# One block for output projection and feed-forward, with the superblocks' ends in another order, in a decoder layer on one Trainium2 core

## What is computed

```python
mixed = jnp.concatenate([y_rwkv, y_pool], axis=-1).astype(x.dtype) @ w_out[layer]
x = x + rms_norm(mixed, post_mix_norm[layer])
h = rms_norm(x, pre_ffn_norm[layer])
f = conv_ffn(h, w_up[layer], conv_w[layer], conv_b[layer], w_down[layer])
x = x + rms_norm(f, post_ffn_norm[layer])
```

## Time and profile before

| | us |
|---|---|
| median of 3 runs | 2393.16 |
| lowest, highest | 2385.60, 2395.46 |
| the profiled execution, its own time | 2396.97 |
| its span, from first to last instruction | 2395.2 |
| TensorE busy in it | 2245.9 (94%) |
| VectorE, ScalarE, GpSimd busy | 1764.1, 1144.1, 1017.4 |
| granted TensorE clock, mean | 0.975 |

### The profile page before, as it was taken

One profiled execution on the slowest core, in us unless ns is written; L12 is line 12 of the kernel. 1 busy time (PEld: TensorE's weight loads), 2 busy tenths in 40 slices (PEclk: granted clock), 3 DMA queues, 4 the chain that ended last, 5 costly groups with the idle time before them and its releaser, 6 DMA issues.

```text
span 2395.2 us, 43619 instructions
## 1 busy us (share of the span) xinstructions
PE 2245.9 (94%) x16652; PEld 1825.7 (76%) x16652; DVE 1764.1 (74%) x1905; ACT 1144.1 (48%) x1794; POOL 1017.4 (42%) x726
## 2 busy tenths in 40 slices
PE   6999999996999989987999999999899999999997
PEld 5777777775878767776888888788678888887885
DVE  2656797984785466767999998656689899976457
ACT  4646565542445444444444444454444444444434
POOL 3646465571333245434677776200136555541000
PEclk9999999997999889998999999999999999999999
DMA  6364555456567357884334344678633233326666
GB/s 186 100 222 131 196 153 184 132 166 164 159 173 195 109 153 237 256 266 145 127 110 144 122 145 136 215 243 257 221 111 114 95 116 100 102 93 206 193 220 211
DMA packets 435787, 395.61 MB, mean 165 GB/s; under 512 B 59516, under 2 KB 352044, under 8 KB 432300
## 3 DMA queue, kind: packets, MB, share of 16 engines
q1 hardware_dynamic: 407772, 343.06, 46.5%
q10 hardware_dynamic: 27856, 50.34, 6.0%
HBM read 266.97 MB, written 126.35 MB: 164 GB/s over the span
## 4 chain that ended last, share of the span: by engine, by line
PE 46%; DVE 3%; DMA 2%; issue 1%; ACT 1%; POOL 1%; SPq 0%; ACTq 0%; DVEq 0%; POOLq 0%
PE late_bank L135 16%; PE late_bank L137 15%; PE late_bank L136 15%; DVE wt_lo L2773 1%; DMA raw<-scratch_td 1%; DVE p_ub L2801 0%; DMA p_keep<-in_w_down 0%; DMA scratch_td<-p_keep 0%; DVE wt_lo L2729 0%; DMA raw<-in_w_down 0%; ACT wt_hi L2613 0%; ACT late_bank L2630 0%; DVE p_ub L2738 0%; DVE p_ub L2804 0%; DVE p_keep L2801 0%
## 5 line engine op out<-in xcount | busy, mean ns | idle before, releaser
L135 PE MATMUL late_bank<-o_hi,wt_hi 128*128 128x512 f32 x1232 | 482.8, 392 | 13.5 <-DVE p_ub L2738 6.1
L136 PE MATMUL late_bank<-o_lo,wt_hi 128*128 128x512 f32 x1232 | 482.1, 391 | 0.0
L137 PE MATMUL late_bank<-o_hi,wt_lo 128*128 128x512 f32 x1232 | 482.0, 391 | 0.0
L428 POOL TENSOR_TENSOR p_w_lo<-p_w_raw,p_w_hi 128x1024 fp32r<-128x1024 f32 x72 | 189.9, 2638 | 223.9 <-ACT p_w_hi L496 223.9
L135 PEld LDWEIGHTS late_bank<-o_hi,wt_hi 128*128 128x128 f32 x1232 | 233.1, 189 | 63.6 <-issue 8.6
L136 PEld LDWEIGHTS late_bank<-o_lo,wt_hi 128*128 128x128 f32 x1232 | 233.0, 189 | 48.7
L137 PEld LDWEIGHTS late_bank<-o_hi,wt_lo 128*128 128x128 f32 x1232 | 232.9, 189 | 48.6
L135 PE MATMUL late_bank<-wt_hi 128*128 128x512 f32 x616 | 242.3, 393 | 16.2 <-DVE wt_lo L2773 15.2
L2493 POOL TENSOR_TENSOR tsum<-raw 128x512 f32<-128x512 f32 x43 | 102.9, 2394 | 363.5 <-DMA out<-tsum 195.0
L136 PE MATMUL late_bank<-wt_lo,wt_hi 128*128 128x512 f32 x616 | 240.8, 391 | 0.0
L137 PE MATMUL late_bank<-wt_hi,wt_lo 128*128 128x512 f32 x616 | 240.7, 391 | 0.0
(11 more groups left out here) (314 smaller groups left out, 4613.1 us busy)
## 6 DMA issues: line engine op xcount, KB each, us to landing
raw<-in_w_up SPq DMA_DIRECT2D x88, 512.0 KB, 5.1
p_w_raw<-in_w_in SPq DMA_DIRECT2D x72, 512.0 KB, 3.9
scratch_a<-p_keep SPq DMA_DIRECT2D x22, 1280.0 KB, 4.6
raw<-scratch_a SPq DMA_DIRECT2D x104, 256.0 KB, 2.9
raw<-scratch_td SPq DMA_DIRECT2D x60, 256.0 KB, 3.6
p_keep<-scratch_a SPq DMA_DIRECT2D x50, 256.0 KB, 2.9
scratch_a<-p_keep SPq DMA_DIRECT2D x44, 256.0 KB, 2.0
raw<-in_w_down SPq DMA_DIRECT2D x44, 256.0 KB, 3.9
```

What stands on the lines that cost most here:

```text
L135: nc.tensor.matmul(out, lhs_hi, rhs_hi, start=start, stop=False, skip_group_check=again)
L136: nc.tensor.matmul(out, lhs_hi, rhs_lo, start=False, stop=False, skip_group_check=again)
L137: return nc.tensor.matmul(out, lhs_lo, rhs_hi, start=False, stop=stop, skip_group_check=again)
L428: nc.gpsimd.tensor_tensor(w_lo[i][:, :, :], w_raw[i][:, :, :], w_hi[i][:, :, :].bitcast(F32), ALU.subtract).then_inc(s_wl, 1)
```

## The change

Both phases become one block (`phase_out_and_ffn`): `mix_out_programs` returns the five programs, which run ahead of the feed-forward's own on each engine, with no barrier or credit block between; the feed-forward's semaphores are credited by SP behind the second tile.

```diff
+            body(0, 0)
+            body(1, 1)
+            for s in credited:
+                sp.sem_inc(s, ONE)
+            for t in range(2, N):
+                body(t, t % 2)
             begin_next()
```

```diff
-                    sp.wait_ge(s_op, ONE + N)
+                sp.wait_ge(s_wl, ONE + 1)
                 for ph in range(EARLY_OPERANDS, OPERANDS):
+                    if ph == 5:
+                        store_quarters(sp, N // 2 - 2)
+                        sp.wait_ge(s_op, ONE + N)
...
+                if t == N - 1:
+                    for k in range(KT):
+                        for n in range(HALF):
+                            last = nc.tensor.matmul(bank[:, 2 * p + n, :], m_hi[p][:, k, :], w_lo[:, k, n * TB:(n + 1) * TB],
+                                                    start=k == 0, stop=False)
+                    last.then_inc(s_wl, 1)
...
+                if t == N - 1:
+                    for ph in (3, 4):
+                        unit_high(ph)
+                        operand_high(ph)
+                    first_copy()
                 act.wait_ge(s_x2, ONE + t + 1)
...
+                if t == N - 1:
+                    unit_high(5)
+                    operand_high(5)
                 act.wait_ge(s_rc, ONE + t * 2 + 2)
```

```diff
+                if p and t < N - 1:
+                    second_root(t, p)
                 if 2 < t <= N // 2 + 1 and p:
                     first_low((t - 3) // 2)
...
                         else:
                             load_step(sup, 0)
                             load_step(sup, 1)
+                        if sup == 0 and u == 0:
+                            mix.store_quarters(sp, N_TILES // 2 - 1)
+                            for p in range(2):
+                                sp.wait_ge(mix.x_stored[p], ONE + N_TILES * 8)
+                                sp.wait_ge(mix.pieces_stored[p], ONE + PIECES * 8)
+                        if sup == 0 and u == 1:
+                            sp.wait_ge(s_qst, ONE + QUARTERS)
+                            load_piece(0)
...
-                        if begins(n) and ph == 0:
+                        if begins(n) and ph == 4:
+                            mix.transposes(pe, N_TILES - 1, 1)
+                        if begins(n) and ph == 5:
+                            pe.wait_ge(mix.turned, ONE + N_TILES)
```

```diff
+        ORDER = (2, 3, 0, 1)
...
-                            piece_sums(h - 2)
+                            piece_sums(h - 1)
...
-                    if ph == PH - 1 and f % 2 and f < 2 * TT:
-                        norm(sup, 0, f // 2)
+                    if ending(sup) and e == RUN:
+                        for t in range(TT):
+                            norm(sup, 0, t)
+                    elif not ending(sup) and ph == PH - 1 and 0 < f <= 2 * TT:
+                        if f % 2:
+                            scaled(sup, 0, f // 2)
+                        else:
+                            added(sup, 0, f // 2 - 1)
...
                 for t in range(TT):
                     last_combine(SUPERS - 1, t)
-                for t in range(TT):
                     norm(SUPERS - 1, 1, t)
```

```diff
+        LAST_PARTS = {14 + 4 * f: f for f in range(FP)}
+        RUN = STEPS - FP
...
+                def last_product(sup):
+                    ph = PH - 1
+                    for t in range(TT):
+                        pe.wait_ge(s_es, ONE + sup * 5 * TT + 2 * TT + t + 1)
+                        for f in range(FP):
+                            if t == 0:
+                                pe.wait_ge(s_ol, ONE + PH - EARLY_OPERANDS + KQ * PH + f + 1)
+                            hi, lo = whole(f, o_hi), whole(f, o_lo)
+                            end = split_matmul(nc, bank[:, BASE[ph] + t, :], hi[:, t * P:(t + 1) * P], lo[:, t * P:(t + 1) * P],
+                                               hi[:, TB:2 * TB], lo[:, TB:2 * TB], False, f == FP - 1, True)
+                        end.then_inc(s_db if t < TT - 1 else s_dp, 1)
```

686 lines of the change are left out of this document (380 added, 306 removed).

## The result

The changed kernel takes **2360.2 us** (median of 4 runs, 2355.37 to 2364.81), the kernel before beside it 2393.26 (4 runs, 2385.6 to 2395.46): ratio 0.986, 95% interval 0.9839 to 0.9881. The forecast was 2346.0 in 2336 to 2359. The sign is right; the size falls short by 14.2 us, and the range misses by 1.2.

What follows compares the result with a forecast made beforehand. TensorE, busy 2245.9 of 2395.2 us, was taken as the bound, so only its waits, low clock and the tail could be won. Six terms sum to 47.2 us, giving 2346.0 against the median 2393.16, range 2336 to 2359.

Steps and rivals of the forecast that it cites:

- Part 1: Output projection, odd tiles: an earlier second reciprocal on VectorE removes four TensorE waits for the scaled tile, -5.8 us.
- Part 2: Projection's end and first unit: the stop between phases goes, 44.5 us becomes 29.5, -15 (bounds -23.7 and -10).
- the second unit near 1091: End of the walk past the projection: the second unit begins near 1091 us instead of 1106.
- queue rival: The full DMA queue, not the block, sets the projection's boundary: -10 there, 2351 us in all; chance 0.17.
- Part 3: First superblock's 77 steps: earlier pieces and a norm cut in two, 223.2 to 215.9 us, -7.3 (-5 to -8.5).
- the first term: First superblock's steps: last piece's store no longer precedes the third step load; its 4.6 us wait goes, 3.8 expected.
- Part 4: Between the superblocks: tiles 2 and 3 first, addition ahead of the norm, -10.5 us (bounds -5.6 and -13).
- backlog rival: VectorE's packed units move the start waits by a unit, 5 and 2 us back, 2353 us; chance 0.13.
- Part 5: Second superblock's last product: step operands loaded and split earlier, four waits at the end go, -2.3 us.
- the ring was not choked: Slower rival, second superblock's steps: early last parts hold back step loads, +63 us, 2409; chance 0.02.
- Part 6: Tail behind the last matmul: norms tile by tile cut 14.5 us to 8.2, -6.3 (-5 to -7).

Runs made afterwards that it cites:

- u1: Changed kernel with VectorE's second reciprocal of odd tiles back behind the copies and the turn; 2365.58 us, ratio 0.9885.
- q1: Changed kernel with the second unit's raw weights loaded ahead of operand 6 instead of behind it; 2347.58 us, ratio 0.9798.
- e1: Changed kernel with the last pair's sums on VectorE moved behind the first addition of the second unit; 2354.57 us, ratio 0.9835.
- n1: Changed kernel with the last tile pair's sums on VectorE cut to one column, giving a wrong result; 2356.61 us, ratio 0.9852.
- gn: g1 with the last tile pair's sums on VectorE also cut to one column, giving a wrong result; 2349.75 us, ratio 0.982.
- h1: g1 with the load queue reordered: second unit's raw weights, sums' store, operands 5 and 6, then small parameters; 2349.58 us, ratio 0.9817.
- o1: Changed kernel with the tiles of the steps in the old order 0, 1, 2, 3; 2359.33 us, ratio 0.9858.
- p1: Changed kernel with the pieces of the down projection's weight sums one pair of units later again; 2356.35 us, ratio 0.9839.
- e2: Changed kernel with ScalarE's store of the first superblock's fourth tile behind the copies of the next unit's first weights; 2354.10 us, ratio 0.9817.
- u2: Changed kernel with the second superblock's last product back in eleven ring steps, norm halves between, no early parts; 2367.99 us, ratio 0.9886.
- g1: q1 with the 512 KB load of the last norm's gain also moved later, into the second unit; 2351.09 us, ratio 0.9819.

## Why the prediction was wrong in size

The miss of 14.2 us (2346.0 to 2360.2) has three parts: 5.5 from the parts of the sum (47.2 forecast, 41.7 in stretches A to F), 3.1 from ahead of stretch A, and 5.6 from where the profiled executions lie among the others: I set the sum against an execution 3.8 us above its median, and the one after stands 1.8 below its own. The last two are scatter, and the forecast had no term for it; without them its sum would have missed by 5.5 us and its range would have held.

*Part 1: right.* -7.1 for -5.8; u1 brings back four waits. The rest is TensorE's own busy time in A, 168.6 us before and 167.4 after, for which the sum had no term.

*Part 2: the step that failed, -15 forecast, -10.5 measured.* Its first half went better than my walk. Counted from the projection's end, operand 5 was copied after 13.7 us (I had 14.5), product 6 began after 24.3 (26.5), and the second unit after 27.0 (29.5). But I let the walk end there. The mis-sized term is "the second unit near 1091", after which I counted no loss: the next unit's raw weights stood last on the crowded queue, the sums I had moved in stood ahead of the additions, and the second unit lost 6.9 us (33.9 of B's 434.1 lie ahead of the 400.2 for 21 units, and 33.9 - 27.0 = 6.9; 5.46 of it waited, the rest at the lower clock). q1 shows the queue's part, 3.6 of them. e1, n1 and gn show the sums' part to be under 1 us, by place or by amount. The other 3.3 us I can't assign: with the weights first (q1) operand 6 is late, in h1's order GpSimd's sums run beside VectorE's low halves, and every such version keeps B at 429.5 to 431.6. So the **queue rival** came nearest: it gave -10 and named "the first unit's raw weights among them"; it was the second unit's. That its figure fits within 0.5 us is partly luck, since it is the sum of a first unit that came 2.5 us sooner than I had it and a second that lost 6.9. Its reason, volume, is only half shown: order gained 3.6 us, and taking out 512 KB that stood behind the late operand gained nothing more. The Trainium skill (Trainium Kernel Development and Optimization, "Key Constraints") says that all queues run on one set of engines, and this trace's DMA share of 1.00 to 1.09 between 1065 and 1080 agrees. What I drew from it, that loads set sooner gain nothing, doesn't fit: operands 3 and 4 were copied 1.0 and 3.4 us behind the projection's end, 11.9 and 15.9 before.

*Part 3: -5.6 for -7.3.* The start waits are 3.8 us, as forecast. The end waits are 2.3 us where I left 0.3: a norm in two halves fits the ring, but GpSimd's sums, moved beside them by part 4, make VectorE's 1.2 us instructions 2.3 (o1, without them, has C at 214.6). By waits and clock, C's 5.6 us are 1.9 of start waits (5.7 to 3.8), 1.1 of end waits (3.4 to 2.3) and 2.4 of clock: 0.83 in 1506.1 to 1520 before, behind the one long wait, 1.00 after. My reason for the first term is too simple: p1 puts the piece's store back ahead of the load, which brings 1.0 us of start waits (4.8 us) and 0.6 us of C, within the noise. The kernel before had the same store and 5.7 us of waits because there it came later still. Both kernels issue the load 3 us behind the store; but GpSimd's four piece sums, which the store waits for, took 5.7 us before (1501.56 to 1507.26) and 4.9 in p1 (1484.62 to 1489.54), and began 4.5 us ahead of the first step instead of 5.4. These two make up the 1.6 us between the two loads; why the sums began and ran later, no run shows.

*Part 4: -8.6 for -10.5.* The chain was as read, and by o1's trace the order is worth more than I gave it. The terms for what is left were both wrong, and it is luck that they nearly cancel: I put 0.4 us ahead of the first product, where there are 2.77, with the clock at 0.78 in 1709 to 1715 on top, and 2.6 us for a wait further on, where there is none. The sum also forgot its own 0.4: 13.1 - 0.4 - 2.6 is 10.1. e2 shows the backlog rival in small: with ScalarE out of the way, VectorE's combine is late by 1.63.

*Part 5: -3.6 for -2.3*, the ring was not choked: no wait at the eleven new parts. The four waits went, but not for the reason given, that no norm stands between low halves: u2, with the norm's halves between them, has none of the four either, and its E is 0.4 us longer. The term was right and its reason was not; the cut in two is the likely one, which no run undoes alone. *Part 6: -6.4 for -6.3.*

The range took one rival at a time, on top of a placing that I treated as exact. Part 2's 4.5 us and the shortfall of parts 3 and 4 came together, and so did 8.7 us of scatter (3.1 ahead of A, 5.6 from where the profiled executions lie); each alone was inside.

## What to carry to other kernels

When a barrier is taken out, walk on until the next unit of the same kind is in step again: what was hidden behind the barrier shows up there, and the load that is issued last in the burst is the first suspect. In a full queue look first at what stands ahead of the late load: moving one of these loads gained 3.6 us here, taking out one that stood behind it gained nothing. A wait that got shorter is no gain by itself; ask whether the load came sooner or the engine later. A forecast for a median needs the scatter of single executions in its range, beside the doubts about the mechanism.

## What the runs showed of the hardware that I had not expected

**A tiny VectorE instruction beside GpSimd costs like a large one.** A 128x4 subtraction took 1.25 us where a GpSimd sum ran (1.60 us from 1079.49 on), and 0.17 us behind it. The Trainium skill (SBUF - State Buffer, "Who interferes with whom") says the later one of two such instructions blocks until the other is through; the 1.25 us fit that, and a slowdown in proportion to size does not.

**Most of the scatter lies ahead of the changed part.** The first transposes of stretch A came at 879.6 us in one profiled execution and at 891.9 in another, with the same instructions ahead of them in all the versions, and at 881.3 and 891.9 in two versions on the same chip; behind it, untouched stretches moved by 1.7 us at most (B of u1), over 1470 us. Both phases ahead have a share: TensorE's last matmul of the input projection began at 535.9 to 543.6 us, and from there to the first transposes it took 342.7 to 354.6 us. What differs inside these phases stays open.

**Nearly the same wait, another clock.** q1 and g1 wait 1.83 and 2.02 us for the last tile's scaled copy, and then run the same eight transposes and product 5:

```profile
1075.09 1.09 PE L2184 MATMUL late_bank<-p_ident,p_hx 128*128 128x128 f32 x8 [1.83 <-ACT p_hx L2084]
```

```profile
1068.31 1.38 PE L2183 MATMUL late_bank<-p_ident,p_hx 128*128 128x128 f32 x8 [2.02 <-ACT p_hx L2083]
```

From the first transpose to the taps it is 4.39 us in q1, at a granted clock of 1.00, and 5.59 us in g1, where the clock is 0.72. So more than 1 us of a stretch can come from what the clock does behind a wait of 2 us. It need not stay in the sum: here the next wait, for operand 6, was shorter by as much.
